# Order of copies and exponentials on ScalarE, and the output copies moved from VectorE to ScalarE, in a hybrid decoder layer

## The reference, cut to what matters

```python
h = x @ w_in                     # q, k, v of 8 heads, 4 pooling groups, 2 gates
for each head, each block of 128 queries:      # causal, with ALiBi bias
    a = softmax(q1 k1 + bias) - lam * softmax(q2 k2 + bias)
    o = a @ v;  o = rms_norm(o, subln_g) * (1 - lam_init)
merged = g_attn * (o @ w_attn_proj) + g_pool * (pool(p) @ ...)
y = layer_norm(alpha * x + merged @ w_out)
for each token, each of 8 retrieval heads:     # 16384 experts, product keys
    scores -> top 16 of the sums of two top-16 lists -> idx, sc
    gate = softmax(sc)
    ffn += sum over 16: gate * gelu(u[idx] . y) * v[idx]
out = layer_norm(alpha * y + ffn)
```

## Time and profile before

| | |
|---|---|
| median of three runs | 3325.46 us |
| the profiled execution | 3328.37 us, span 3326.4 us |
| busy: TensorE, VectorE, ScalarE, GpSimd | 2798.8, 2475.0, 1162.4, 1324.7 us |
| DMA | 1244.97 MB, mean 374 GB/s |
| ACT_TABLE_LOAD | 107 at L879, 63 at L864, 43 at L782, 1 at L902 |

### The profile page before, as it was taken

One profiled execution on the slowest core, in us unless ns is written; L12 is line 12 of the kernel. 1 busy time (PEld: TensorE's weight loads), 2 busy tenths in 40 slices (PEclk: granted clock), 3 DMA queues, 4 the chain that ended last, 5 costly groups with the idle time before them and its releaser, 6 DMA issues.

```text
span 3326.4 us, 30256 instructions
## 1 busy us (share of the span) xinstructions
PE 2798.8 (84%) x8368; PEld 1442.0 (43%) x8368; DVE 2475.0 (74%) x5989; ACT 1162.4 (35%) x3421; POOL 1324.7 (40%) x1248
## 2 busy tenths in 40 slices
PE   9999999999976799889988989867877777777776
PEld 7776565445433345444444544323433222222222
DVE  2316788896888778997799877888788676667664
ACT  2202555453122233445454522232323333333332
POOL 1101354554334343444454544344444444444432
PEclk9999999999998999999999999889989999999999
DMA  5635999999999999999999999999999999999997
GB/s 190 245 136 199 383 388 373 383 362 368 419 399 407 421 420 407 405 361 332 336 370 370 364 420 420 375 388 420 420 420 418 421 416 421 416 414 417 420 415 311
DMA packets 205223, 1244.97 MB, mean 374 GB/s; under 512 B 23680, under 2 KB 36992, under 8 KB 73600
## 3 DMA queue, kind: packets, MB, share of 16 engines
q0 software_dynamic: 147456, 1073.81, 79.8%
q1 hardware_dynamic: 56592, 169.11, 13.6%
q10 hardware_dynamic: 1008, 0.14, 0.0%
HBM read 1228.81 MB, written 14.16 MB: 374 GB/s over the span
## 4 chain that ended last, share of the span: by engine, by line
PE 41%; DMA 30%; DVE 18%; issue 6%; ACT 4%; POOL 1%; SPq 0%; POOLq 0%; DVEq 0%; ACTq 0%
DMA ring<-uv,idx 30%; PE r_o L1579 15%; PE w_ps L1373 14%; DVE ring L1306 8%; DVE z_e L1258 3%; PE w_ps L1421 2%; PE r_o L1550 1%; PE w_ps L1550 1%; PE w_ps L1516 1%; PE w_ps L1458 1%; PE w_ps L1493 1%; DVE e L1022 1%; POOL ring L706 1%; PE r_o L1493 1%; PE r_o L1516 1%
## 5 line engine op out<-in xcount | busy, mean ns | idle before, releaser
L706 POOL DMA_INDIRECT ring<-uv,idx x1024 | 1172.3, 1145 | 1722.9 <-PE r_o L1579 1231.0
L1579 PE MATMUL r_o<-ring,diag 128*128 128x512 f32 x2936 | 1445.6, 626 | 403.9 <-ACT diag L892 388.1
L1306 DVE CUSTOM_DVE_ANT_0 ring<-ring,ytok 128x1024 f32<-128x1024 f32 x768 | 937.1, 1221 | 234.1 <-DMA ring<-uv,idx 232.7
L1579 PEld LDWEIGHTS r_o<-ring,diag 128*128 128x128 f32 x2936 | 539.7, 195 | 1131.9 <-ACT diag L892 590.0
L879 ACT ACTIVATE gel<-dot 128x2 f32<-128x2 f32 x512 | 104.0, 203 | 1608.9 <-DVE dot L1306 1605.3
L1373 PE MATMUL w_ps<-x,w 128*128 128x384 f32 (+1 forms) x2112 | 655.4, 456 | 9.7 <-DMA x<-xT 5.9
L1373 PEld LDWEIGHTS w_ps<-x,w 128*128 128x128 f32 x2112 | 395.9, 192 | 230.0 <-issue 59.1
L1306 DVE CUSTOM_DVE_ANT_0 ring<-ring,zn 128x1024 f32<-128x1024 f32 x256 | 313.3, 1224 | 211.3 <-DMA ring<-uv,idx 211.3
L1258 DVE SCALAR_TENSOR_TENSOR z_e<-ring,coef,z_e 128x1024 f32<-128x1024 f32 x290 | 371.7, 1282 | 0.2 <-ACT coef L883 0.2
L892 ACT ACTIVATE diag<-ident,coef 128x128 f32<-128x128 f32 x734 | 262.8, 387 | 0.0
L883 ACT ACTIVATE coef<-gel,gate 128x1 f32<-128x1 f32 x1024 | 246.0, 287 | 16.8
(11 more groups left out here) (199 smaller groups left out, 2331.3 us busy)
## 6 DMA issues: line engine op xcount, KB each, us to landing
w<-w_in SPq DMA_DIRECT2D x132, 512.0 KB, 3.6
wq<-wq SPq DMA_DIRECT2D x46, 512.0 KB
wc<-w_branch SPq DMA_DIRECT2D x24, 768.0 KB, 8.4
ring<-uv,idx POOLq DMA_INDIRECT x1024
wo<-w_out SPq DMA_DIRECT2D x24, 512.0 KB, 10.7
xs<-x SPq DMA_DIRECT2D x8, 512.0 KB
out<-yn_e SPq DMA_DIRECT2D x8, 512.0 KB, 11.6
x<-xT SPq DMA_DIRECT2D x16, 192.0 KB, 4.0
```

Source lines behind the costliest of these rows:

```text
L706: nc.gpsimd.indirect_dma_start(out=ring[t % RING][:], out_offset=None, in_=a["uv"], in_offset=bass.IndirectOffsetOnAxis(ap=idx[:, slot:slo ...
L1306: nc.vector.tensor_tensor_reduce(ring[r][:, 0:D], ring[r][:, 0:D], y_of(n)[:], 1.0, 0.0, ALU.mult, ALU.add, dot[:, slot:slot + 1]).then_in ...
L1579: ins = nc.tensor.matmul(o_ps[n % 2][half][:], diag[(u - 1) % DIAGS][:], ring[t % RING][:, D + half * HALF:D + (half + 1) * HALF], start=s ...
```

## The change

`transposed` moves from VectorE to ScalarE, as an activation Copy with the gain as its scale. In ScalarE's stage the order of the generators becomes units, pooling, `turned_out`, `transposed`, `exponents`, the rest as before: of what is due in one slot, both copies now come ahead of the attention's exponentials. The retrieval's exponentials become a generator of their own, merged behind the stages; `exponent_at(G)` gives the due slot 16 G - 10, or a slot up to five later in which an attention exponential of group 1 or 2 falls due. `invert` and `share` move from slots 16 G - 7 and 16 G - 6 to 16 G - 3 and 16 G - 2. ScalarE's first exponential waits for one more VectorE instruction, the scaling of the gain.

```diff
+def exponent_at(g):
+
+    begin = TOPK * g - SEARCH_AHEAD + 14
+    steps = [step_at(j, k) + DO_EXP[j] for j in range(1, NG) for k in range(NSTEPS[j])]
+    return min([slot for slot in steps if begin <= slot < begin + 6], default=begin)
...
     @block.scalar
...
+        def transposed(g):
+            for k in range(NSTEPS[g]):
+                m = STEP0[g] + k
+                h, j = k // GTS[g], k % GTS[g]
+                yield step_at(g, k) + DO_OT[g] + 1
+                act.wait_ge(on_turned, m + 1)
+                if g == 1 and k == 0:
+                    act.wait_ge(q_unit, 4)
+                if g == 1 and k == GTS[g] * 4:
+                    act.wait_ge(q_unit, HP * g)
+                nc.scalar.activation(o_all[g][:, h, j * P:(j + 1) * P], out_bank(g)[:, 0:P], ACT.Copy,
+                                     scale=o_gain).then_inc(o_ready, 1)
...
-            return merged(units(g), pooling(g), exponents(g), turned_out(g), head_norm(g), first_norms(g), flipped(g),
-                          queries(g), scores_out(g))
+            return merged(units(g), pooling(g), turned_out(g), transposed(g), exponents(g), head_norm(g), first_norms(g),
+                          flipped(g), queries(g), scores_out(g))
...
+        def shares():
+            for g in range(1, RH * TT):
+                yield exponent_at(g)
+                exponent(g)
...
-        act.wait_ge(lam_step, 2)
+        act.wait_ge(lam_step, 3)
...
-        advance = woven(all_stages(stage))
+        advance = woven(merged(all_stages(stage), shares()))
...
-                ahead = SLOTS * n + slot + SEARCH_AHEAD
-                if ahead % TOPK == 14 and ahead // TOPK < RH * TT:
-                    exponent(ahead // TOPK)
                 advance(SLOTS * n + slot + GROUP)
...
     @block.vector
...
-        def transposed(g):
...
-                nc.vector.tensor_scalar(o_all[g][:, h, j * P:(j + 1) * P], out_bank(g)[:, 0:P], o_gain, None,
-                                        ALU.mult).then_inc(o_ready, 1)
...
-            return merged(pooling(g), logits(g), outputs(g), transposed(g), branches(g), residuals(g), first_norms(g))
+            return merged(pooling(g), logits(g), outputs(g), branches(g), residuals(g), first_norms(g))
...
-                if j == 1 and 2 <= g <= RH * TT:
+                if j == 5 and 2 <= g <= RH * TT:
                     invert(g - 1)
-                if j == 2 and 2 <= g <= RH * TT:
+                if j == 6 and 2 <= g <= RH * TT:
                     share(g - 1)
```

## The result

The changed kernel takes 3339.36 us (median of 6 runs, 3336.24 to 3347.63) against 3324.88 us for the kernel before: 14.5 us slower by the medians (0.44%); the ratio is estimated at 1.0049, with a 95% interval of 1.0039 to 1.0059. One of the executions of the kernel before that were taken beside the first four experiments took 9985.5 us and counts in no ratio. I had forecast 3316.4 us and a range that ended at 3332.

A forecast was written before the change was run, and what follows sets the result against it. TensorE bounds stretch A; in C no engine is full and they hand waits to each other. Terms -9.8 - 2.3 + 4.3 + 1.5 - 0.7 - 2.1 = -9.1 us, from median 3325.5 to 3316.4 us; range 3299 to 3332.

The forecast's parts named there:

- aT ahead of the exponentials: ScalarE's second copy in stretch C: TensorE's values stop waiting for it, gain cut by the next diagonal's slack; -9.8 us.
- Exponentials later: ScalarE in C: both copies delay the attention's exponentials by 0.57 us; seven counted at 0.6; +4.3 us.
- Output copy: Moved from VectorE to ScalarE: in C most waits only move to the reciprocal, -2.3 us; in A -2.1 us.
- C: Stretch of slots 320 to 479, 536 us, no engine full; forecast to end some 7 us shorter.
- A: Stretch of slots 0 to 127, 441 us, bound by TensorE; shorter waits for the output copy, -2.1 us.
- Retrieval exponentials: Sharing table loads with the attention's, 214 to 190 loads, mostly hidden by idle time on ScalarE; -0.7 us.
- Elsewhere it costs nothing: Retrieval exponentials moved by up to three slots outside the 12 shared places: 0 us.
- Coefficients and diagonals behind on ScalarE: Queued behind the exponentials, they come 0.3 us later; five steps had no slack at the diagonal; +1.5 us.
- Prologue: Outside A and C, such as group 0's 16 steps: no effect expected.
- rival 2: Slower: in group 2's steps ScalarE holds the exponentials for late output transposes; 3344 us, or 3338 with two thirds; chance 0.13.
- Rival 1: In C the 9.8 us gain ends as TensorE's wait for VectorE's logits; 3326 us; chance 0.31.
- Rival 4: ScalarE's table loads are on the path, so 30.8 us go; 3295 us; chance 0.04.

The follow-up runs named there:

- the first four experiments: Runs that take the change apart against the kernel before: T alone 3333.7 us, O alone 3324.5, X alone 3323.4, T and X 3333.9.
- T alone: Kernel before with only the copies aT put ahead of the attention's exponentials on ScalarE: 3333.7 us, ratio 1.0025.
- filler: Kernel before with two small unread copies on ScalarE ahead of each pair of group 2's exponentials, 24 times: 3334.6 us, ratio 1.0031.
- O alone: Kernel before with only the output copy moved to ScalarE, ahead of the exponentials, aT still behind them: 3324.5 us, ratio 0.9998.
- T and X: The whole change except the output copy, which stays on VectorE: 3333.9 us, ratio 1.0026 against the kernel before.
- X alone: Kernel before with only the retrieval's exponentials behind the attention's, invert and share four slots later: 3323.4 us, ratio 0.9996.
- combo_no_x: Output copies on ScalarE, group 2's exponentials first, aT behind the exponentials, retrieval's exponentials unmoved: 3304.1 us, ratio 0.9934 against the kernel before.

## Why the prediction was wrong

*aT ahead of the exponentials, forecast -9.8 us: the step that failed.* The copy ended the values' wait as forecast, and I had rightly cut the gain by the next diagonal's slack (that wait rose from 9.3 to 24.1 us, by the 14 us I had named). But I took the diagonal for the only thing late next. The bank shared by values and block transposes, and VectorE's copy L1053 that frees it, is in the code and I didn't follow it: the wait of the block transposes grew by 20 us, from 5.0 to 24.8 in T alone, as much as the 19.7 that ended at the values. T alone measured +9 us. By the filler's rate, worked out below, 7 of them are the later exponentials, so the term itself was 0 to +2 and not -9.8.

*Exponentials later, forecast +4.3: mis-sized twice.* First the delay. I had 0.57 us a step, 13 in all (and seven at 0.6 are 4.2). From the start of the copies to that of the table load the kernel after has 0.63 to 0.86 us in 16 of the 21 steps with both copies, as most copies aT are wider than the one of 0.36 us that I took. In the other five ScalarE also waits for the output transpose, 0.5 to 1.7 us and 5.4 together, where I had seen two such steps. It is 22.6 us in all 23 steps. Second, what counts of it. I let it count for seven of 23 steps, from the chain's shares by line; the filler shows 0.64 counting. By that rate T's own delay (11.0 us in 23 steps) is 7.0 of its 9 us, and the other 2 are within its interval (5 to 12). The same rate on 22.6 us gives 14.4, the change's whole loss; that is in part luck, since in O alone the exponentials are held up too, by 16 us with ScalarE's waits, and nothing is lost; there VectorE is rid of its copies and of 19.3 us of waits for them.

*Output copy, forecast -2.3 in C and -2.1 in A: right in kind.* The wait moved to the reciprocal; by itself it is 0 (-4 to +2 by the interval). On top of T and X it cost 5.4 us, which I had not foreseen. The exponentials start later by then, 22.6 us in all for T's 11.0, but why that costs here and not in O alone is open.

*Retrieval exponentials, forecast -0.7: right.* -1.4 us with an interval of -4.3 to +1.3. "Elsewhere it costs nothing" was wrong in one place: slot 6, where ScalarE isn't idle. Slots 0 to 31 took 119 us for 116 in X alone.

*Coefficients and diagonals behind on ScalarE, forecast +1.5:* no run has this by itself.

*A, forecast -2:* 441 us became 440.5. Prologue: nothing, as forecast.

*The rivals.* The time was that of rival 2 (3338 to 3344), its sign and place too, and a part of its cause: ScalarE does hold the exponentials for late output transposes in C, but for 5.4 us in five steps, not in more than half of them. The larger part is the work in front of the exponentials, aT's above all. Rival 1 had the gain end as waiting for VectorE's logits; that wait did not grow (16.7 us before, 16.3 in T alone, 14.6 in the change). Rival 4, the table loads on the path, is refuted by x_only and by combo_no_x. The Trainium skill ("ScalarE: Activation LUTs", section "Table sets: the hidden batching unit") has the rule to batch calls by table set; the change followed it with 24 loads fewer, and in x_only that moved nothing, as the loads lie in idle time. Of my tests for being wrong none named the outcome: C was to shrink by 7 us or to stay, and grew by 16. VectorE's wait at the reciprocal, "30 or more", came true with 56.7 and told nothing: O alone has 47.8 without a loss.

## What to carry to other kernels

When engines hand a loop's steps to each other, the wait that looks longest (TensorE's for aT) need not be the one that pays. Ask which instruction the next two or three waits hang on, and follow the buffers that two uses share; if it is the same one, what is put in front of it has its price, however short. A filler of known length in front of the suspect measures its worth, and moving the suspect to the front of its queue tests it from the other side. A tie in an order written by due slots is a decision: here the exponentials behind aT cost 9 us, and first of all that was due they brought 9 us. Parts measured one at a time need not add up: the output copies cost nothing alone and 5.4 us beside T.

## What the runs showed that I had not expected

Output copies behind the exponentials cost 24.5 us, though the scores' bank had been waited for in six steps only (11 us). In stretch A, where TensorE is 95% busy, its wait for the bank grew by 22.6 us, and slot 128 came 21.8 us late: there nearly all of it counts. And 24 table loads of 1.283 us, 30.8 us of ScalarE's time, are worth nothing measurable in two different orders.
